# A channel mixer with three buffers for its second weight table and three for each kind of gathered row

## What is computed

```python
def blk(xb):
    q = (xb @ wq).reshape(PEER_BLOCK, PEER_HEADS, PEER_QDIM)
    s1 = einsum('bhd,nd->bhn', q[..., :half], k1)      # 8 heads, 128 keys
    s2 = einsum('bhd,nd->bhn', q[..., half:], k2)
    t1, i1 = top_k(s1, 16); t2, i2 = top_k(s2, 16)
    cand = t1[..., :, None] + t2[..., None, :]
    top, sel = top_k(cand, 16)                         # 16 of 16,384 experts a head
    gate = softmax(top)
    act = gelu(einsum('bd,bhkd->bhk', xb, u_tab[idx])) * gate
    return einsum('bhk,bhkd->bd', act, v_tab[idx])
```

## Time and profile before

| what | value |
|---|---|
| runs | 4609.35, 4609.68, 4616.98 us; median 4609.68 |
| profiled execution | 4606.3 us, span 4604.0 us |
| granted TensorE clock, mean of the span | 0.911 |
| busy: PE, PEld, DVE, ACT, POOL | 3857.9, 2856.7, 2775.5, 1030.0, 1592.2 us |
| DMA | 1201.42 MB, 261 GB/s over the span |
| queue q0 (POOL's, the gathers in it) | 570.77 MB |
| queue q1 (SP's loads) | 534.63 MB |

### The profile page before, as it was taken

The page is one execution under the profiler, slowest core; times in us unless marked ns, Lnnn a source line. Parts: engine busy times, 40 slices in busy tenths (PEclk is TensorE's granted clock), DMA queues, the critical chain, the costliest instruction groups (busy, mean ns, idle before and its releaser), DMA issues. The chain is left out here.

```text
span 4604.0 us, 50577 instructions
## 1 busy us (share of the span) xinstructions
PE 3857.9 (84%) x17166; PEld 2856.7 (62%) x17166; DVE 2775.5 (60%) x6132; ACT 1030.0 (22%) x2824; POOL 1592.2 (35%) x1334
## 2 busy tenths in 40 slices
PE   9788857887998899979889488768989899888885
PEld 4577834445876677757667344456767677666664
DVE  0255522222797877767777422345997877667766
ACT  0133111111121355401101112211212555200101
POOL 0012023331053365645555000000342766555552
PEclk9898968988999899989999799969999899999997
DMA  3100167664587899989999364404788999899995
GB/s 122 40 19 13 42 188 199 193 189 144 179 320 270 317 416 417 413 332 400 392 401 386 138 236 145 162 19 148 268 289 301 388 417 416 344 391 395 396 395 194
DMA packets 387502, 1201.42 MB, mean 261 GB/s; under 512 B 34340, under 2 KB 173221, under 8 KB 359277
## 3 DMA queue, kind: packets, MB, share of 16 engines
q0 software_dynamic: 159856, 570.77, 32.8%
q1 hardware_dynamic: 198718, 534.63, 32.1%
q10 hardware_dynamic: 28672, 92.81, 5.1%
HBM read 1108.45 MB, written 85.11 MB: 259 GB/s over the span
## 5 line engine op out<-in xcount | busy, mean ns | idle before, releaser
L2082 PE MATMUL peer_bank<-region,peer_v 128*128 128x288 f32 x4096 | 1031.6, 416 | 157.5 <-DMA peer_v<-in_v 121.0
L1967 POOL DMA_INDIRECT peer_ru<-in_u_rows,peer_expert x512 | 763.1, 1490 | 1128.9 <-DVE peer_dot L2245 817.3
L2035 PE MATMUL peer_bank<-peer_xT,peer_u 128*128 128x288 f32 x4096 | 1041.8, 412 | 42.3 <-ACT peer_hidden L2148 42.3
L2082 PEld LDWEIGHTS peer_bank<-region,peer_v 128*128 128x128 f32 x4096 | 798.7, 195 | 390.4 <-DMA peer_v<-in_v 127.6
L2035 PEld LDWEIGHTS peer_bank<-peer_xT,peer_u 128*128 128x128 f32 x4096 | 779.2, 193 | 252.3 <-issue 45.6
L2235 DVE SCALAR_TENSOR_TENSOR y<-peer_rv,peer_weight,y 128x1024 f32<-128x1024 f32 x512 | 655.7, 1281 | 188.6 <-ACT peer_weight L2098 116.6
L1975 POOL DMA_INDIRECT peer_rv<-in_v_rows,peer_expert x512 | 617.2, 1205 | 288.4 <-DVE y L2235 149.6
L2245 DVE CUSTOM_DVE_ANT_0 peer_ru<-peer_ru,x 128x1024 f32<-128x1024 f32 x512 | 623.2, 1217 | 24.6 <-DMA peer_ru<-in_u_rows,peer_expert 22.1
L2096 ACT ACTIVATE peer_act_g<-peer_dot 128x1 f32<-128x1 f32 x512 | 103.4, 202 | 1214.3 <-DVE peer_dot L2245 1203.6
L2371 DVE TENSOR_TENSOR region<-region,peer_bank 128x288 f32<-128x288 f32 x496 | 219.6, 450 | 166.8 <-PE peer_bank L2082 161.9
L1198 POOL DMA_DIRECT2D mla_vals<-in_cache_ckv x256 | 140.0, 547 | 313.2 <-PE mla_bank L1300 229.0
(11 more groups left out here) (506 smaller groups left out, 4448.5 us busy)
## 6 DMA issues: line engine op xcount, KB each, us to landing
peer_u<-in_uT SPq DMA_DIRECT2D x128, 1024.0 KB
peer_v<-in_v SPq DMA_DIRECT2D x64, 2048.0 KB
mlstm_w_in<-in_w_in_o SPq DMA_DIRECT2D x30, 1792.0 KB, 7.3
mla_keys<-in_keysT SPq DMA_DIRECT2D x256, 144.0 KB, 4.8
scratch_early<-peer_hidden ACTq DMA_DIRECT2D x64, 576.0 KB
scratch_grids<-region ACTq DMA_DIRECT2D x24, 1536.0 KB
region<-scratch_grids SPq DMA_DIRECT2D x32, 1152.0 KB
region<-scratch_early SPq DMA_DIRECT2D x64, 576.0 KB
```

Source lines behind the costliest of these rows:

```text
L1967: pool.indirect_dma_start(ru[:, n % U_ROWS, :], None, u_rows, bass.IndirectOffsetOnAxis(ap=expert[:, T, k:k + 1], axis=0)).then_inc(ru_in[ ...
L2035: mm = mmul(bank[:, 4 + i % 2, 0:TD], u[:, h % URING, i % 2, k, :], xT[:, k, :], start=k == 0, stop=k == KD - 1)
L2082: mm = mmul(bank[:, SUM_BANKS[m % 6], 0:TD], v[:, g % 2, j, c * P:(c + 1) * P], w[:, g % 2, j, :], start=j == 0, stop=j == GI - 1)
```

## The change

Three edits. The v table of the sums stage gets `VRING` = 3 buffers; `ru` and `rv` get three each. In the memory of a partition one v buffer is 16 KiB and one row buffer 4 KiB, so one v buffer more and four row buffers less leave the total as it was. The first three parts of v are issued at the first turn, and in the sums stage v of group g+1 is issued before w of group g, behind the same wait.

```diff
-U_ROWS, V_ROWS = 5, 5
+U_ROWS, V_ROWS = 3, 3
+VRING = 3
...
-        v = sb("v", [P, 2, GI, D])
-        wq = v[:, :, :, :].rearrange("p a b c -> p a (b c)").rearrange("p a (k n) -> p a k n", k=KD)
+        v = sb("v", [P, VRING, GI, D])
+        wq = v[:, 0:2, :, :].rearrange("p a b c -> p a (b c)").rearrange("p a (k n) -> p a k n", k=KD)
...
                 def load_v(g):
-                    if g >= 2:
-                        sp.wait_ge(sums, KD * (g - 1))
+                    if g >= VRING:
+                        sp.wait_ge(sums, KD * (g - VRING + 1))
...
                     if what == "turn" and i == 0:
-                        load_v(0)
-                        load_v(1)
+                        for g in range(VRING):
+                            load_v(g)
...
+                    if VRING <= g + 1 < NGRP:
+                        load_v(g + 1)
                     if g >= 2:
                         sp.wait_ge(sums, KD * (g - 1))
                     sp.dma_start(w[:, g % 2, :, :].rearrange("p a b -> p (a b)"), hidden_dram[g]).then_inc(h_in[g % 2], 16)
-                    if g >= 2:
-                        load_v(g)
...
-                    pe.wait_ge(v_in[g % 2], 16 * (g // 2 + 1))
+                    pe.wait_ge(v_in[g % VRING], 16 * (g // VRING + 1))
```

More of the change, by code:

```diff
@@ L1887, in peer_mix @@
         list_ok = sem("experts_listed")
-        u_in, v_in = [sem(f"u_loaded{i}") for i in range(URING)], [sem(f"v_loaded{i}") for i in range(2)]
+        u_in, v_in = [sem(f"u_loaded{i}") for i in range(URING)], [sem(f"v_loaded{i}") for i in range(VRING)]
         dots, gelus, sent_h = sem("dots"), sem("gelus"), [sem(f"hidden_sent{i}") for i in range(2)]
@@ L1913, in load_v @@
                 def load_v(g):
-                    if g >= 2:
-                        sp.wait_ge(sums, KD * (g - 1))
+                    if g >= VRING:
+                        sp.wait_ge(sums, KD * (g - VRING + 1))
                     else:
                         sp.wait_ge(q_ok, 2 * NQ)
-                    sp.dma_start(v[:, g % 2, :, :].rearrange("p a b -> p (a b)"), v_dram[:, g * GI * D:(g + 1) * GI * D]).then_inc(v_in[g % 2], 16)
+                    sp.dma_start(v[:, g % VRING, :, :].rearrange("p a b -> p (a b)"), v_dram[:, g * GI * D:(g + 1) * GI * D]).then_inc(v_in[g % VRING], 16)
                 def load_wq(i):
@@ L2081, in _ @@
                         for j in range(GI):
-                            mm = mmul(bank[:, SUM_BANKS[m % 6], 0:TD], v[:, g % 2, j, c * P:(c + 1) * P], w[:, g % 2, j, :], start=j == 0, stop=j == GI - 1)
+                            mm = mmul(bank[:, SUM_BANKS[m % 6], 0:TD], v[:, g % VRING, j, c * P:(c + 1) * P], w[:, g % 2, j, :], start=j == 0, stop=j == GI - 1)
                         mm.then_inc(sums, 1)
```

## The result

The changed kernel takes 4658.77 us (median of 6 runs, 4645.65 to 4665.55) against 4613.97 for the kernel before in the same comparison (4609.35 to 4623.02): ratio 1.0087, 95% interval 1.0068 to 1.0106. It is slower by some 45 us; the forecast was 4636, range 4590 to 4700.

A forecast was written before the change was run, and what follows sets the result against it. VectorE was taken to bound the rank stage, TensorE the final, full DMA engines mark and sums; per layer -1 (sums) + 0 (early v) + 9 (rank) + 5 (mark) = +13, +26 for two layers: 4636 us, range 4590 to 4700.

The forecast's parts named there:

- The step of rows 6 and 7: Rank stage: with three buffers, v rows landing 9 to 11 us after issue come 2 to 4 us late; +9 us a layer.
- The third part of v at the turn: First turn, final stage: loading v's third buffer early costs 0, up to 2 us a layer, because a late row meets slack.
- The bound from rows 1: Mark stage: 0 if bytes decide, to 18 us a layer at 5% idle, 393 GB/s for 414; +5 taken.
- Forecast -1: Sums stage: -1 us a layer, near the lower sum of two opposed effects, because bytes set the cycle.
- The relief by fewer rows: Sums stage stall: at most four rows instead of ten still land, taking 2.1 MB, 5 us, off the queue.
- the 1.8 of the weighing: Sums stage: w now lands last, so four weighing operations follow the last load, 1.8 us more in a stall.
- Its most for that room: Sums stage: perfect filling can give at most some 3 us in each of seven cycles, 20 us a layer.
- The signs set for it: Sums stage: stalls of 6 to 9 us remain about every fourth group; stalls at every second would break the forecast upward.
- the gates crawl because of their pieces: Sums stage: gates come in 768-byte pieces and crawl beside rows in 4,096-byte pieces, 1.93 MB moved against 5.93.
- rows lose nothing: Rival, chance 0.22: rank and mark stages stay, only the sums' -1 a layer is left; 4608 us.
- the row ring becomes the bound: Rival, chance 0.15: mark stage loses 18 us a layer, sums 11, rank 9; 4686 us; sign: mark stage over 365 us.
- the stalls of the sums stage go: Rival, chance 0.18: sums gain 20 us a layer, rank stage loses 9; 4588 us; sign: sums cycles under 70 us.

## Why the prediction was right or wrong

**The direction and the rank stage were right.** The step of rows 6 and 7 took place as worked out. In the changed kernel, the load of wq, the gather of v for pick 10 and its addition:

```profile
1332.62 0.38 SPq L1924 DMA_DIRECT2D peer_v<-in_wq  x1
...
1333.96 0.94 POOL L1976 DMA_INDIRECT peer_rv<-in_v_rows,peer_expert  x1 [0.30 <-issue]
...
1344.17 1.28 DVE L2236 SCALAR_TENSOR_TENSOR y<-peer_rv,peer_weight,y 128x1024 f32<-128x1024 f32 x1 [2.27 <-issue]
```

The row's last packet comes at 1343.1, 9 us after its issue (forecast 9 to 11), and the addition is 2.27 us late (forecast 2 to 4). The stage costs 6.2 and 9.6 us, forecast 9. VectorE's waits there are four after v rows, 5.3 us, and one after a u row, 0.8; TensorE restarts 5.6 us later, counted from the first unit:

```profile
1439.35 1.30 PE L2036 MATMUL peer_bank<-peer_xT,peer_u 128*128 128x288 f32 x2 [18.13 <-ACT peer_hidden L2149]
```

The kernel with three u and five v rows loses nothing in this stage: it is the v rows, as forecast.

**The final stage had no term for the rows.** It costs 6.8 and 7.1 us. The prediction saw the repeated wait for ScalarE of the earlier trace rows and took it for a slack that hides a late row. But the picks stand behind that wait, not ahead of it, and VectorE's addition behind it is what frees a v buffer. In the changed kernel:

```profile
1497.96 1.28 DVE L2236 SCALAR_TENSOR_TENSOR y<-peer_rv,peer_weight,y 128x1024 f32<-128x1024 f32 x1 [17.91 <-ACT peer_weight L2099]
...
1499.51 1.67 POOL L1976 DMA_INDIRECT peer_rv<-in_v_rows,peer_expert  x1 [17.31 <-DVE y L2236]
...
1511.36 1.28 DVE L2236 SCALAR_TENSOR_TENSOR y<-peer_rv,peer_weight,y 128x1024 f32<-128x1024 f32 x1 [6.22 <-issue]
```

With five buffers this row (pick 35) was asked for ahead of the wait, at 1429.9 in the kernel before. With three it goes out after it, lands some 11 us later and is waited for 6.22 us. The delay reaches TensorE behind the next turn, where a unit waits 6.04 us for ScalarE instead of 1.70. The third part of v at the turn, priced at 0 in the same step, did cost nothing: three rows alone, without it, lose the same 7 us.

**The mark stage was mis-sized.** The term was +5 with 18 as its high end; measured 20.6 and 17.6. The prediction looked for the loss in the moments in which the row queue is empty and took a DMA share of at least 0.98 as a sign that there are few. The share over the stage is 1.00, and the stage lost all the same. Stretches of 20 us of the changed kernel:

```profile
1680.00:1700.00 20.00, 19.42 (x99) 15.71 (x98) 15.48 (x25) 11.24 (x34) 12.91 (x11) 1.00 0.96 370
1720.00:1740.00 20.00, 19.09 (x96) 15.46 (x95) 16.27 (x27) 10.84 (x35) 14.30 (x10) 1.00 0.94 351
1760.00:1780.00 20.00, 17.83 (x90) 14.54 (x89) 13.46 (x22) 10.24 (x31) 11.66 (x10) 0.98 1.02 417
```

The kernel before has 411 to 421 GB/s in every such stretch from 1620 to 1940; for example:

```profile
1720.00:1740.00 20.00, 18.56 (x94) 15.04 (x93) 15.15 (x25) 11.19 (x34) 14.14 (x10) 1.00 1.02 420
```

That fewer rows ahead mean a shorter wait was right: from the packets, a u row takes 7.7 us on average from issue to landing in this stage, before 12.6. But it lies ready 3.3 us before its use on average, before 5.9, and a mean of 3.3 leaves the waits shown above. The bound from rows 1 (5% of idle time, 393 GB/s) was the better estimate than its cheap end: it is what happened, 394.

**The sums stage had the right parts and the wrong balance.** Forecast -1, measured -8.2 and -11.2. The relief by fewer rows (5 us a stall in the prediction) is -9.6 and -9.2 a layer when done alone. The new order costs more than a third v buffer gives: the two together, with five rows, make the stage 1 and 4 us longer, where that buffer with w first makes it 16 and 10 shorter. With v ahead the first three stalls of layer 0 grow by 1.1 to 2.7 us, near the 1.8 of the weighing; in layer 1 one of three does. The prediction had no term for rows that come late in this stage, which now take 76.9 us of VectorE. ("At most four rows instead of ten" should be six, three of each kind; its 2.1 MB are right for four fewer.) It let the two effects cancel because bytes set the cycle; but the cycles of the kernel before stand at 383 as well as 401 GB/s, and a rate that varies leaves room. Its most for that room, 20 us a layer, was passed: three buffers for v, w and the gates gained 22.0 and 21.4. The signs set for it were wrong too: there were no stalls of 6 to 9 us every fourth group but small ones at nearly every second, and that did not break the forecast upward, since they sum to 47.8 us where seven long ones summed to 60.7. That the gates crawl because of their pieces is borne out in small part: half the piece hardly slowed them, and 12 of their 30 us they stand behind a part of v. Larger pieces were not tried, and what holds them up beside the rows stays open.

**The sum**, 26 us against 48.5 in the profiles and 45 in the medians, stayed inside its range in part by luck: two errors of opposite sign met, 7 us a layer forgotten in the final stage and some 14 too little in the mark stage, against some 9 too little gained in the sums.

**The rivals.** That rows lose nothing was wrong. That the row ring becomes the bound was right about the mark stage (18 us), and its sign came true: the 350 us of that stage became 370, over its 365. Its other sign, a DMA share clearly under 1, showed in single stretches (0.94) and not over the stage (1.00), and it was wrong about the sums, which gained. That the stalls of the sums stage go came true, but in other kernels: not by the third v buffer in the order of the change, but by that buffer with w issued first (4591 us; that this rival has 4588 is chance, since its sum holds 9 us of loss in the rank stage, which this kernel does not have) and by third buffers for w and the gates (4572 us). In the changed kernel one cycle of layer 0 is under the 70 us set as its sign, at 69.5. The full DMA engines in the gap, had been taken as evidence against it. What filled them was mostly what was waited for; the queues in these eight us of the kernel before, first 2114 to 2118, then 2118 to 2122:

```profile
q1 hardware_dynamic: 138, 1.30, 77.3%
q0 software_dynamic: 131, 0.46, 29.0%
...
q1 hardware_dynamic: 175, 1.52, 90.3%
q0 software_dynamic: 42, 0.12, 7.7%
```

SP's w and v came behind the gates, and these were slow while rows filled the engines in the 20 us ahead: a full gap shows that the load is under way, and not that an earlier start would not have helped. The Trainium skill, "Perfetto Trace Analysis", section Optimization Strategy, takes a repeating gap for a possible want of buffers. Here the trace agrees only with a condition on the order of the queue: a third v buffer with v ahead of w made it 1.0025, the same buffer with w ahead 0.9950, and third buffers for w and the gates besides 0.9903.

## What to carry to other kernels

A buffer that a wait names may not be all that is late: ask what stands in the queue ahead of it, and do not let the load that a new buffer allows earlier stand in front of one that is needed sooner. Before paying for a buffer with another ring's, look for memory that is idle in that stage; here the ring of u was, and the kernel that used it kept all rows and became 1% faster. A lead that lands in time on average (3.3 us early in the mark stage) can still cost some 19 us a layer where the time to land varies, and a row that can be asked for only behind a long wait comes late whatever the average.

## What the runs showed of the hardware

In the stretches of 20 us and more shown here and in the earlier trace rows, a DMA share of 0.94 to 1.00 stood beside 351 to 398 GB/s and a share of 1.02 or 1.03 beside 401 to 420: near 1 a step of 0.02 in the share went with some 20 GB/s, so the bytes a second have to be read with it.

Issuing a load can hold SP itself. With the gates in half pieces, SP's loads ahead of group 8:

```profile
2097.25 14.48 SPq L1948 DMA_DIRECT2D region<-scratch_grids  x1
2111.77 13.66 SPq L1952 DMA_DIRECT2D region<-scratch_early  x1
2125.47 0.43 SPq L1918 DMA_DIRECT2D peer_v<-in_v  x1
```

The second half of the gates took 14.48 us to issue and w behind it 13.66, where such issues take 0.43 and 0.32 us in the kernel before; v went out 13 us later for it. That cost little: by the packets this v landed 5.4 us behind the gates, and 7.8 us in the kernel before. Whether the number of pieces under way is what holds SP was not tried.
